# Two layers on one core: four unit buffers for the expert weights and one pipeline of eight head pairs

## What is computed

```python
def first_block(x, mem, ...):
    h = x
    h = h + _mixer(h, ...)              # gated linear attention and differential attention
    h = h + _cross_attention(h, mem, ...)
    h = h + _hier_moe(h, ...)
    return h

def _hier_moe(h, ...):                  # 32 experts in 4 groups, each token goes to 2
    def expert_block(args):
        xb, e = args
        hid = jax.nn.silu(xb @ w_gate[e]) * (xb @ w_up[e])    # 1024 x 512 each
        return hid @ w_down[e]                                # 512 x 1024

def hybrid_layer(x, mem, g_in, w_in, b_merge, g_mem, w_mem_kv, w_up_moba, w_up_dsa, w_up_cross, w_out):
    z = rmsnorm(x, g_in) @ w_in
    (mq, mk, mv, mg, dq, dk, dv, dg, iq, ik, iw, xq, xg, glog) = split(z)
    ya = (moba_attention(rope(mq), rope(mk), mv) * silu(mg)) @ w_up_moba     # 8 heads of 64
    yb = (dsa_attention(rope(dq), rope(dk), dv, rope(iq), rope(ik), iw) * silu(dg)) @ w_up_dsa
    yc = (cross_attention(xq, xk, xv) * silu(xg)) @ w_up_cross               # 4 heads of 128
    gates = sigmoid(glog + b_merge)                                          # 3 branches
    u = gates[0] * ya + gates[1] * yb + gates[2] * yc
    return x + u @ w_out

out = rmsnorm(hybrid_layer(first_block(x, mem, ...), mem_2, ...), g_final)
```

## Time and profile before

| | |
|---|---|
| median of 3 runs | 1154.57 us (1149.91 to 1155.44) |
| profiled execution | 1153.48 us |
| its span | 1151.8 us |
| PE busy | 892.0 us, 77% |
| DVE busy | 458.9 us, 40% |
| ACT busy | 315.6 us, 27% |
| HBM read | 290.25 MB |
| expert weights, from their first issue to their last products | 278.87 to 794.66 us |
| second layer, from its first transposes on PE to the end | 807.19 to 1151.8 us |

### The profile page before, as it was taken

One profiled execution on the slowest core, in us unless ns is written; L12 is line 12 of the kernel. 1 busy time (PEld: TensorE's weight loads), 2 busy tenths in 40 slices (PEclk: granted clock), 3 DMA queues, 4 the chain that ended last, 5 costly groups with the idle time before them and its releaser, 6 DMA issues.

```text
span 1151.8 us, 13540 instructions
## 1 busy us (share of the span) xinstructions
PE 892.0 (77%) x5425; PEld 616.2 (53%) x5425; DVE 458.9 (40%) x843; ACT 315.6 (27%) x505; POOL 21.6 (2%) x34
## 2 busy tenths in 40 slices
PE   5999978889775667576757575754899869899986
PEld 4777866777641212121313121311787769799985
DVE  4668664553430202020202020101566855645484
ACT  3646634543100000000000000002234335455322
POOL 1020000000000000000000000000000000000000
PEclk9999989999796968887888797888899979999999
DMA  7643444424389999999999999996345324443350
GB/s 256 194 150 107 156 174 146 144 75 150 161 335 422 422 422 421 422 422 422 422 421 422 423 421 423 421 421 230 106 157 174 109 74 150 144 141 129 138 179 37
DMA packets 75196, 291.99 MB, mean 254 GB/s; under 512 B 9522, under 2 KB 9868, under 8 KB 50572
## 3 DMA queue, kind: packets, MB, share of 16 engines
q1 hardware_dynamic: 72812, 288.48, 64.5%
q10 hardware_dynamic: 2336, 2.84, 0.7%
HBM read 290.25 MB, written 1.05 MB: 253 GB/s over the span
## 4 chain that ended last, share of the span: by engine, by line
DMA 32%; issue 32%; PE 27%; DVE 5%; ACT 2%; SPq 2%; POOL 0%; DVEq 0%; POOLq 0%; ACTq 0%
DMA ring<-in_w_e_down 16%; DMA ring<-in_w_e_up 15%; PE bank L1943 5%; PE bank L1945 5%; PE bank L1944 5%; PE bank L2250 4%; PE bank L2269 4%; SPq L581 2%; DVE ring_rounded L1169 1%; ACT ring_rounded L748 1%; PE bank L2185 1%; DVE ring_rounded L1155 1%; PE bank L1890 1%; PE bank L2156 1%; PE bank L2201 1%
## 5 line engine op out<-in xcount | busy, mean ns | idle before, releaser
L1169 DVE TENSOR_TENSOR ring_rounded<-ring,ring_rounded 128x2048 fp32r<-128x2048 f32 x80 | 183.3, 2292 | 198.7 <-ACT ring_rounded L748 198.5
L2250 PE MATMUL bank<-ring,main 128*32 128x512 f32 x1024 | 155.5, 764 | 99.6 <-DMA ring<-in_w_e_up 75.2
L748 ACT ACTIVATE ring_rounded<-ring 128x2048 fp32r<-128x2048 f32 x80 | 153.1, 1916 | 223.7 <-PE bank L1945 223.7
L1944 PE MATMUL bank<-ring_rounded 128*128 128x256 f32 (+1 forms) x512 | 161.7, 316 | 0.0
L2250 PEld LDWEIGHTS bank<-ring,main 128*32 128x32 f32 x1024 | 38.9, 135 | 209.4 <-issue 136.9
L1945 PE MATMUL bank<-ring_rounded 128*128 128x512 f32 x368 | 145.6, 396 | 0.0
L2269 PE MATMUL bank<-ring,main 128*32 128x512 f32 x512 | 87.1, 842 | 57.5 <-DMA ring<-in_w_e_down 57.5
L1943 PE MATMUL bank<-uT_rounded,ring_rounded 128*128 128x256 f32 x352 | 103.5, 294 | 5.1 <-issue 5.1
L1944 PEld LDWEIGHTS bank<-ring_rounded 128*128 128x128 f32 x512 | 100.8, 197 | 5.2
L1945 PE MATMUL bank<-uT_rounded,ring_rounded 128*128 128x256 f32 x352 | 101.2, 288 | 0.0
L1943 PE MATMUL bank<-ring_rounded,uT_rounded 128*128 128x512 f32 x224 | 89.3, 399 | 7.2 <-issue 4.3
(11 more groups left out here) (266 smaller groups left out, 1118.6 us busy)
## 6 DMA issues: line engine op xcount, KB each, us to landing
ring<-in_w_e_gate SPq DMA_DIRECT2D x64, 1024.0 KB, 16.8
ring<-in_w_e_up SPq DMA_DIRECT2D x64, 1024.0 KB, 16.7
ring<-in_w_e_down SPq DMA_DIRECT2D x64, 1024.0 KB, 18.8
ring<-in_w_in SPq DMA_DIRECT2D x46, 1024.0 KB, 5.0
ring<-in_w_ckv SPq DMA_DIRECT2D x8, 1024.0 KB, 4.9
ring<-in_w_o SPq DMA_DIRECT2D x4, 1024.0 KB, 5.0
ring<-in_w_cq SPq DMA_DIRECT2D x4, 1024.0 KB, 4.9
ring<-in_w_mem_kv SPq DMA_DIRECT2D x4, 1024.0 KB, 5.2
```

Source lines behind the costliest of these rows:

```text
L748: a.activation(rounded(hi_half(h)), raw_half(name, h), ACT.Copy).then_inc(hi_made, 1)
L1169: v.tensor_tensor(rounded(raw), raw, as_f32(hi_half(h)), ALU.subtract).then_inc(split_made, 1)
L1944: mm(dst, left[0], right[1], start=False, stop=False, skip_group_check=True)
L2250: last = mm(bank[2 + part][on, :], xg3[:, h * (KC // 2) + k, on], weight_unit(u % 3, e, KC)[:, k, :], start=h + k == 0, stop=h * (KC // 2) ...
```

## The change

**Experts.** `UNIT_BUFFERS = 4`: unit number 6p + u of a pair of quads goes to buffer (6p + u) % 4, for which the loops of SP and PE now run over pairs of quads. The new buffer 2 is in 3 x 8 KB of each partition of `main` from `spare_at`, and for the fourth expert in `uT`; the third of before is buffer 3. SP waits for a `unit_used` that is one less.

```diff
+UNIT_BUFFERS = 4
+            if b == 2 and e == GROUP - 1:
+                piece = uT[:, :, :].rearrange("p c t -> p (c t)")
+            elif b == 2:
+                piece = main[:, spare_at + e * HALF:spare_at + (e + 1) * HALF]
+                    sp.wait_ge(moe.unit_used, of_quad(j, p, UNITS, u - UNIT_BUFFERS + 1))
+                    load_unit(unit_buffer(p, u), experts, w_of, u % 2, chunks)
...
             load_unit(0, range(GROUP), gate_w_of, 0)
-            for e, name in ((0, "co1"), (2, "xv2")):
-                wait_filled(sp, LAST_USE[name])
-                load_unit(1, (e, e + 1), gate_w_of, 1, at=e)
-            load_unit(2, range(GROUP), up_w_of, 0)
+            load_unit(2, range(GROUP - 1), up_w_of, 0)
+            wait_filled(sp, LAST_USE["co1"])
+            load_unit(1, (0, 1), gate_w_of, 1)
+            wait_filled(sp, "logits")
+            load_unit(2, (GROUP - 1,), up_w_of, 0, at=GROUP - 1)
+            wait_filled(sp, LAST_USE["xv2"])
+            load_unit(1, (2, 3), gate_w_of, 1, at=2)
+            load_unit(3, range(GROUP), up_w_of, 1)
...
-            sp.wait_ge(moe.unit_used, UNITS * QUADS)
+            sp.wait_ge(moe.unit_used, UNITS * QUADS - 2)
...
-            with pe.Fori(0, QUADS - 1) as i:
-                experts(moe, i)
-                gather(moe, i + 1)
-                scatter(moe, i)
-            experts(moe, QUADS - 1)
+            with pe.Fori(0, QUADS // 2 - 1) as j:
+                quad(j, 0)
+                quad(j, 1)
+            quad(QUADS // 2 - 1, 0)
+            experts(moe, QUADS // 2 - 1, 1)
```

```diff
+PAIRS = [(kind, pair) for kind in "ms" for pair in range(4)]
+PAIR_BLOCKS = ["xq", "gl0", "gl1", "dg", "xg", "gl2", "gl3", "gl4"]
+for n, ((kind, pair), b) in enumerate(zip(PAIRS, PAIR_BLOCKS)):
+    PSUM_PLAN += [f"{b}_0", f"{kind}pT{2 * pair}", f"{kind}pT{2 * pair + 1}", f"{b}_1"]
+    if n + 1 < len(PAIRS):
+        kind2, pair2 = PAIRS[n + 1]
+        PSUM_PLAN += [f"{kind2}s0_{pair2}", f"{kind2}s1_{pair2}"]
+    PSUM_PLAN += [f"{kind}o{pair}"]
+PSUM_PLAN += ["xs0_0", "xs1_0", "xs0_1", "xs1_1", "gl5_0", "gl5_1", "xpT0", "xpT1", "xo_0", "xo_1"]
+PSUM_PLAN += [f"up0_{c}" for c in range(4)] + ["xpT2", "xpT3", "xo_2", "xo_3"]
+PSUM_PLAN += [f"up{b}_{c}" for b in (1, 2) for c in range(4)]
...
+            for n, b in enumerate(PAIR_BLOCKS):
+                def between(h):
+                    if h == 1:
+                        pair_turn(*PAIRS[n])
+                        if n + 1 < len(PAIRS):
+                            pair_scores(*PAIRS[n + 1])
+                standing(b, stream, before_half=between)
+                pair_out(*PAIRS[n])
+                if n + 1 == len(PAIRS):
+                    x_scores()
...
+            standing("gl5", stream, before_half=first_x)
+            x_out(0)
...
-                dense(f"up{n}", parts(hi, y), [f"up{n}_{c2}" for c2 in range(4)], True)
+                dense(f"up{n}", parts(hi, y), [f"up{n}_{c2}" for c2 in range(4)], True,
+                      None if n else second_x)
+                if n == 0:
+                    x_out(1)
```

More of the change, by code:

```diff
@@ L1099, in _ @@
                     copy(f"xpT{hh}", x_pT[hh % 2])
-                filler(f"gl{4 + hp}")
-            for name in ("up1", "up2", "out0", "out1"):
+            split_hi("up0", [0])
+            x_turned(0)
+            split_hi("up0", [1])
+            block_out("gl5")
+            split_hi("up1", [0])
+            x_turned(1)
+            split_hi("up1", [1])
+            for name in ("up2", "out0", "out1"):
                 split_hi(name)
@@ L1849, in _ @@
+            x_bias(2)
+            x_bias(3)
+            split_lo("up0", [0])
+            x_weights(2)
+            x_weights(3)
+            split_lo("up0", [1])
+            for hh in (0, 1):
+                finish_x(hh)
             for b in range(3):
@@ new lines, in pair_scores @@
+            def pair_scores(kind, pair):
+                q3, k3, _, masks = of_kind[kind]
+                if pair == 0 and kind == "m":
+                    for c in range(2):
+                        wait_drained(pe, f"mqT{c}")
+                        wait_drained(pe, f"mkT{c}")
+                elif pair == 0:
+                    for c in range(2):
+                        wait_drained(pe, f"dqT2_{c}")
+                        wait_drained(pe, f"dkT2_{c}")
+                    pe.wait_ge(selected, 2)
+                scores([f"{kind}s{n}_{pair}" for n in range(2)], q3[:, pair, :], k3[:, pair, :], masks)
```

398 lines of the change are left out of this document (209 added, 189 removed).

## The result

| | before | after |
|---|---|---|
| median | 1152.32 us (1149.91 to 1155.44, 4 runs) | 1135.42 us (1132.92 to 1136.88, 4 runs) |
| span of the profiled execution | 1151.8 us | 1133.6 us |

The ratio is 0.985, with an interval of 0.9814 to 0.9885: 1.5% faster. The forecast was 1134.5 us, made for the profiled execution, which took 1135.30 us. The median of before has one execution more than in the table ahead of the prediction.

What follows compares the result with a forecast made beforehand. The prediction took the experts to be bound by the weight stream and the second layer by PE and its waits. It summed 1153.5 - 9.9 - 9.1 = 1134.5 us, range 1127.5 to 1146.

Steps and rivals of the forecast that it cites:

- Part 1: Experts: a fourth buffer lets one more unit land in the lull before them, everything behind moves up; -9.9 us.
- The border: Between experts and second layer: first transfers issued earlier, rounding still behind the norm; costed at nothing, bounds 0 and 2 us gain.
- Part 2: PE's expert loop, body doubled to pairs of quads, three passes for seven: not fetched again, 0 us.
- The rival with 22%: PE's doubled loop is fetched again, or DVE costs as much: about 8 us more, 1142.5 us; chance 22%.
- Part 3: Second layer's attention as one pipeline of eight pairs: PE waits of 19.4 us and 5.1 us of low clock go.
- Part 4: Second layer: new PE waits at `mv`, fourth cross score bank, `up1`, `up2`; 14.7 us with the low clock.
- The mis-sized term: Second layer: lower PE clock behind two of the new waits, 3.8 and 3.9 us, 1.5 us each, 3.0 in all.
- The slower rival: Expert weight stream loses rate writing `main` or `uT`; all 19 us gone at 405 GB/s, up to 1171.5 us; chance 5%.
- The sum: Whole kernel: the terms -9.9 and -9.1 us taken from 1153.5, giving 1134.5 us.

## Why the prediction was right

- **Part 1, the fourth buffer: -9.9 forecast, -9.6 in the two traces.** The mechanism is shown by the runs with and without the early load, whose last products stand 8 to 9 us apart; over all traces the expert stage is 9.5 us shorter with the early unit. Part of it doesn't show at 780.95, because that execution's first layer ended 1.16 us later. The DMA share of over 0.9 in the lull, forecast until about 303 us, lasted until 308 at 1.02.
- **The border, forecast at nothing with a bound of 2 us of gain: -1.6.** The value lies within the bound, but the cause isn't the one that was weighed. The prediction looked at the rounding of the first weights behind the norm. What moved was PE's branch, which ended last there and no longer does. The row of 8.10 us of "issue" in the trace of before was the hint: DVE's normalized rows were there at 805.57, 1.6 us ahead of the transposes, and no engine's work filled the rest.
- **Part 2, the loop: 0 forecast, and nothing that the runs can tell.** The rival with 22% was over-priced: the loop isn't fetched again, and even twelve packets don't slow the stream measurably.
- **Part 3, waits that go: all seven went,** 19.2 us in the trace for 19.4 (one of the three like 0.74 was 0.60), and the cover of DVE's picks held. The clock through the eight pairs is 1.00.
- **Part 4, waits that come: 2.0, 3.8, 3.9 and 2.0 forecast, 2.02, 3.81, 4.05 and 2.32 measured,** 12.2 us for 11.7. The mis-sized term is the clock: 3.0 forecast for two of them, but three were followed by a low one, 4 x 0.42 behind `mv`, 4 x 0.33 behind the scores, 4 x 0.50 and 4 x 0.16 behind `up1`, 5.6 us. By that the layer should have gained 6.7. It gained 8.2, of which 1.75 is the clock of the first block, which no edit touched; the rest is 6.4. The low clock isn't a fixed price either: behind the same wait of 2.02 us in front of `mv` it is 0.58 to 0.65 in five traces and 1.00 in two.
- The slower rival needed 405 GB/s; the stream is at 421, a quarter of it into `main` and `uT`. The even rate of before could not say so much, since the stream wrote `ring` alone; the changed kernel's does.
- The sum was 19.0 and the spans differ by 18.2; by the medians it is 16.9. That it came so near is in part luck: the low clock cost 2.6 us more than forecast and the first layer ended 1.16 us later, while the border gave 1.6 and the first block's clock 1.75 that were not in the sum. The mechanisms of parts 1 to 4 are those forecast.
- The two parts add up as far as the runs can tell, and so do the waits: one at a time 6, 2 and 10 us by the ratios, and all of them, with that of 1.99 besides, 16.5 to 19.

## What to carry to other kernels

Where a stage is bound by a stream, look for idle queues ahead of it and count in units of buffers what could land there: the gain is the bytes over the rate, and it arrived at the stage's end almost whole, 9.5 us of 9.9. When the order of work is changed under a round-robin plan of banks, list for each new first user who drains the bank before it, and what stands ahead of that drain on its queue: here four such waits took back 12 us and their low clock 5.6, and moving the drain ahead of work that nobody was waiting for, or the new user to another bank, took them away but for 2 us. A wait that is removed is worth its length less the next one in the same place, plus the clock behind it. A single trace tells a stage to 2 or 3 us here: before a remainder of that size is put down to the change, the same stage is looked up in other runs that have the same code there.

## What the runs showed of the hardware that was not expected

- A branch of PE's, during which one packet of its instructions moved, took 6.3 us in three traces with the DMA queues full and 3.6 to 3.9 us in three with them idle (shares of 1.05 and of 0.02 to 0.05). All of the difference lies ahead of the packet. In this kernel it paid to have the weights landed before the branch.
- Twelve packets of instructions, 0.20 MB, in the stream cost nothing measurable, and a loop of four to five packets stays in place over its three passes: none moved between 420 and 675 us.
- The length of a wait alone does not decide the clock behind it: 2.02 us was followed by 0.58 and 2.32 us by 1.00 in one trace, and the same wait of 2.0 us in front of `mv` by 0.58 to 0.65 in five traces and by 1.00 in two. Behind the first block of the second layer, every wait of 3.5 us or more in the fourteen traces was followed by a clock of 0.71 or less in the next 4 us. Why the shorter ones differ stays open.
